# Expert layers with whole fp32 rows and results, gathered pair by pair, with a ring of twelve weight places

## The chip, the cores and the metric

One core of a Trainium2 chip runs the whole program. Its engines are TensorE (PE in the profile; PEld is its weight load), VectorE (DVE), ScalarE (ACT), GpSimd (POOL) and SyncE (SP), which issues the DMAs. The metric is the device time of one execution in microseconds.

## The reference, cut to what matters

Three transformer blocks run one after the other over 256 tokens of width 1024. Each ends in a mixture of experts: a router picks two of 32 experts for every token, and each expert is a gated two-layer product. The first block has narrow experts (hidden width 256), the two others wide ones (512).

```python
def hierarchical_moe_2(x, w_coarse, b_coarse, w_fine, b_fine, w_gate, w_up, w_down):
    ...
    order = jnp.argsort(expert_id)
    tok = order // TOP_K
    sizes = jnp.bincount(expert_id, length=N_EXPERTS_2)
    xs = xt[tok]                                             # gather
    hid = jax.nn.silu(lax.ragged_dot(xs, w_gate, sizes)) * lax.ragged_dot(xs, w_up, sizes)
    ys = lax.ragged_dot(hid, w_down, sizes) * gate.reshape(-1)[order][:, None]
    return jax.ops.segment_sum(ys, tok, num_segments=T)      # scatter
```

The narrow layer (`hierarchical_moe`) computes the same with other names. Everything is fp32. The rest of the program (projections, gated linear attention, delta rule, retention, window attention, a Fourier mixer, norms) is not changed by the diff except in where some buffers lie.

## The kernel before, in words

`stage_packed` (L1633) runs one expert layer. The 32 experts are taken as 16 pairs; each expert has 64 slots (`CAP`), so that a pair fills 128 partitions. For each pair:

- **gather** (L1693): the token rows of the pair are collected by products with a 0/1 matrix `one`. The rows `h` are kept as two tiles, `h_high` (rounded to fp32r by ACT, L1451) and `h_low` (the rest, subtracted by POOL, L1476), each the stationary operand of a product of type fp32r (L1704, L1705). One call gathers a *batch*: four pairs in the narrow layer (moving operand 512 columns), two pairs in a wide one (256 columns). That is 8 row blocks x 2 token halves x 2 parts = 32 products for each batch. ACT copies the result out of PSUM (L1795).
- **gate and up products** (`hidden`, L1708, L1717) in fp32, ACT's Silu (L1800), DVE's product of the two (L1860), a turn of the result by PE (L1769), ACT's copy of it (L1803), the **down product** (L1740).
- the result times the slot's gate is again kept as high (ACT, L1813) and low (DVE, L1870), and **scattered** (L1722): for each of four outputs of 128x512 two fp32r products (L1727, L1728), which DVE adds to `x` (L1834). The scatter of pair p stands in PE's order of pair p+1: outputs 0 and 1 behind the up product, 2 and 3 behind the turn.

PE's written order within pair p is: gate, turn of the gated one-hot (L1757), up, scatter 0 and 1 of pair p-1, turn of hidden (L1769), scatter 2 and 3, gather of the next batch if p is a batch's last pair, down.

The weights stream through a **ring** of places of 2 MB each (`Experts`, L1571). A narrow pair takes 3 such chunks (48 in the layer), a wide pair 6 (96 in the layer). SP issues chunk i when the place of chunk i - ring size has been used (L1616). The ring has 8 places in the narrow layer and 10 in a wide one. Ring places are also used by other stages: the first loads of a layer are issued wherever a place is already free, in `stage_norm`, `stage_fourier` and `stage_out_route` (L1336), the last two behind a wait for the out product (L2577), since `store` holds its weights.

`stage_out_route` computes the output projection (L1396), the residual and norm on DVE, the turned rows (L1404), the router's logits (L1412), a long chain of small DVE operations that picks the experts (L1513 to L1562), and PE's ranking product (L1431). `refine` is a Newton step for a square root.

Of the kernel before, what the change touches and what calls it, by code (L numbers as in the profile page):

```python
# [7 lines left out]
ALU = mybir.AluOpType  # L8
# [3 lines left out]
F32R = mybir.dt.float32r  # L12
I32 = mybir.dt.int32

P = 128
T = 256
# [238 lines left out]
def stage_norm_t(k, tag, src, weight, ahead=None):  # L255

    nc = k.nc
    s_w, s_ss, s_inv, s_rs, s_h, s_t = (k.sem(f"{n}_{tag}") for n in (
        "norm_weight_loaded", "sumsq_done", "inv_done", "rstd_done", "h_done", "turned"))
    scope = ExitStack()  # L260
    k.scope = scope
    ss = k.sb(f"ss_{tag}", [P, NJ])
    inv = k.sb(f"inv_{tag}", [P, NJ])
    rstd = k.sb(f"rstd_{tag}", [P, NJ])
    turned = k.ps(f"turned_ps_{tag}", [P, 4, W])
    rows, wrow = src, None
    if weight is not None:
        rows = k.sb(f"norm_rows_{tag}", [P, NJ, D])
        wrow = k.sb(f"norm_row_{tag}", [P, D])

    with scope, nc.Block() as block:
        @block.sync
        def _(sp):
            if weight is not None:
                sp.dma_start(wrow[:], weight.broadcast_to([P, D])).then_inc(s_w, 16)
            if ahead is not None:
                ahead(sp)

        @block.scalar
        def _(act):  # L280
            if weight is not None:
                for j in range(NJ):
                    nc.scalar.activation(rows[:, j, :], src[:, j, :], ACT.Square,
                                         accum_out=ss[:, j:j + 1]).then_inc(s_ss, 1)
                act.wait_ge(s_inv, 1)
                nc.scalar.activation(rstd[:], inv[:], ACT.Sqrt).then_inc(s_rs, 1)

        @block.vector
        def _(dve):
            o = Order(dve, k.order["dve"])  # L290
            if weight is not None:
                dve.wait_ge(s_ss, NJ)
                o(nc.vector.tensor_scalar(ss[:], ss[:], 1.0 / D, EPS, ALU.mult, ALU.add))
                nc.vector.reciprocal(inv[:], ss[:]).then_inc(s_inv, 1)
                dve.wait_ge(s_rs, 1)
                refine(nc, o, rstd[:], ss[:], inv[:])
                dve.wait_ge(s_w, 16)
                for j in range(NJ):
                    nc.vector.scalar_tensor_tensor(out=rows[:, j, :], in0=src[:, j, :], scalar=rstd[:, j:j + 1],
                                                   in1=wrow[:], op0=ALU.mult, op1=ALU.mult).then_inc(s_h, 1)  # L300
            for b in range(4):
                j, c0 = b // 2, 4 * (b % 2)
                dve.wait_ge(s_t, b + 1)
                dst = k.hT[:, c0:c0 + 4, j * P:(j + 1) * P]
                got = turned[:, b, :].rearrange("p (c t) -> p c t", c=4)
                nc.vector.tensor_copy(dst, got)
            o.restart()

        @block.tensor
        def _(pe):  # L310
            for b in range(4):
                j, c0 = b // 2, 4 * (b % 2)
                if weight is not None:
                    pe.wait_ge(s_h, j + 1)
                for c in range(4):
                    last = nc.tensor.transpose(turned[:, b, c * P:(c + 1) * P],
                                               rows[:, j, c0 + c:D:KC], k.table("ident"))
# [958 lines left out]
def stage_norm(k, tag, gain, bias, ahead=None, out=None):  # L1276
# [6 lines left out]
    with scope:  # L1283
        g = k.sb(f"gain_{tag}", [P, D])
        b = k.sb(f"bias_{tag}", [P, D])
        stats = k.sb(f"stats_{tag}", [P, NJ, 2, 6])
        mv, v, inv, rs = (k.sb(f"{n}_{tag}", [P, NJ, 2]) for n in ("mean_var", "var_eps", "inv", "rstd"))
        with nc.Block() as block:
            @block.sync
            def _(sp):  # L1290
                sp.dma_start(g[:], gain.broadcast_to([P, D])).then_inc(s_ld, 16)  # L1291
                sp.dma_start(b[:], bias.broadcast_to([P, D])).then_inc(s_ld, 16)
# [15 lines left out]
            def _(dve):  # L1308
# [9 lines left out]
                def rows(j):  # L1318
# [4 lines left out]
                    o(nc.vector.scalar_tensor_tensor(out=xj, in0=xj, scalar=mv[:, j, 0:1], in1=g[:],  # L1323
# [241 lines left out]


CHUNK = 2 * KC * H1
RING = 10


class Experts:  # L1571
# [1067 lines left out]
```

## Time and profile before

| | us |
|---|---|
| runs | 2005.18, 2002.22, 2004.66 (median 2004.66) |
| the profiled execution | 2002.44 |
| its span | 2000.5 |
| PE busy in the span | 1785.5 (89%) |
| DVE / ACT / POOL busy | 674.3 / 427.7 / 83.4 |
| HBM read | 577.39 MB, 290 GB/s over the span |

The narrow expert layer runs from about 554 to 808 us of the span, the first wide layer from about 986 to 1437, the second from about 1533 to 1984. PE's records of consecutive matmuls overlap, so that the spacing of their starts, and not their mean duration, tells what one costs. An fp32 product shows as two records, an fp32r product and a turn as one. An engine that waits for a DMA is shown with the tile that the DMA writes.

### The profile page before, as it was taken

The numbers are of one execution on the slowest core, as the hardware profiler recorded it, in microseconds if no ns is written. First come the engines' busy times: TensorE is split into PE (matmuls) and PEld (weight loads), VectorE is DVE, ScalarE is ACT, GpSimd is POOL, SyncE is SP. The second block draws the span as 40 slices with busy tenths as digits, with TensorE's granted clock in tenths as the row PEclk, the third lists the DMA queues.
The fourth block names the chain that finished last, engine by engine and source line by source line (L and its number), as shares of the span: only waits on it lengthen the run. The fifth ranks groups of instructions, "written<-read, shape, count | busy, mean of one in ns | idle before, by whom it ended". The sixth has DMA issues, their size and how long they took to land. (4 is left out here: it accounts for less than half of the span.)

```text
span 2000.5 us, 20692 instructions
## 1 busy us (share of the span) xinstructions
PE 1785.5 (89%) x8544; PEld 952.9 (48%) x8544; DVE 674.3 (34%) x1347; ACT 427.7 (21%) x713; POOL 83.4 (4%) x66
## 2 busy tenths in 40 slices
PE   7999897895799999799799999899597999998995
PEld 6884454695455555456434443333254344442331
DVE  3657333446223334443412222122303122221223
ACT  2321224352222221222211111111112111111110
POOL 0000001311100000120100000000001000000000
PEclk9999998797899999899799999999897999999998
DMA  5345320004669996432999999999793999999995
GB/s 194 127 162 178 123 88 4 0 1 194 243 249 398 403 419 266 144 155 73 384 423 423 423 423 423 423 424 423 299 375 143 424 423 423 423 423 424 423 423 232
DMA packets 100017, 581.49 MB, mean 291 GB/s; under 512 B 23947, under 2 KB 26251, under 8 KB 34893
## 3 DMA queue, kind: packets, MB, share of 16 engines
q1 hardware_dynamic: 87997, 577.81, 70.8%
q10 hardware_dynamic: 11920, 2.26, 0.6%
q8 instruction: 73, 1.20, 0.2%
q14 instruction: 27, 0.22, 0.0%
HBM read 577.39 MB, written 2.62 MB: 290 GB/s over the span
## 5 line engine op out<-in xcount | busy, mean ns | idle before, releaser
L1717 PE MATMUL up_ps_l<-pool,hT 128*64 128x512 f32 x640 | 143.5, 597 | 13.4 <-DMA pool<-in_expert_w_up 13.4
L1717 PE MATMUL gate_ps_l<-pool,hT 128*64 128x512 f32 x640 | 141.4, 593 | 6.6 <-DMA pool<-in_expert_w_gate 5.3
L446 PE MATMUL proj_ps<-pool,hT 128*128 128x512 f32 x320 | 140.2, 598 | 5.6 <-DVE pool L684 5.6
L1740 PE MATMUL y_ps_l<-pool,hidden_l 128*64 128x512 f32 x640 | 142.6, 596 | 2.3 <-ACT hidden_l L1803 1.4
L1870 DVE SCALAR_TENSOR_TENSOR y_low_l<-y_ps_l,slot_gate_l,y_high_l 128x512 fp32r<-128x512 f32 x64 | 47.1, 751 | 251.2 <-ACT y_high_l L1813 251.2
L438 PE MATMUL proj_ps<-hT,pool 128*128 128x256 f32 x512 | 111.9, 380 | 0.0
L1860 DVE TENSOR_TENSOR hidden_l<-hidden_l,up_ps_l 128x512 f32<-128x512 f32 x32 | 22.0, 688 | 245.2 <-PE up_ps_l L1717 245.2
L438 PEld LDWEIGHTS proj_ps<-hT,pool 128*128 128x128 f32 x512 | 96.9, 190 | 14.8 <-issue 1.8
L446 PEld LDWEIGHTS proj_ps<-pool,hT 128*128 128x128 f32 x320 | 61.4, 192 | 81.3 <-issue 74.7
L1717 PEld LDWEIGHTS gate_ps_l<-pool,hT 128*64 128x64 f32 x640 | 45.5, 137 | 98.4 <-issue 87.6
L1717 PEld LDWEIGHTS up_ps_l<-pool,hT 128*64 128x64 f32 x640 | 43.6, 137 | 99.4 <-issue 77.8
L1813 ACT ACTIVATE y_high_l<-y_ps_l,slot_gate_l 128x512 fp32r<-128x512 f32 x64 | 44.0, 687 | 203.1 <-PE y_ps_l L1740 199.6
L1740 PEld LDWEIGHTS y_ps_l<-pool,hidden_l 128*64 128x64 f32 x640 | 43.8, 137 | 88.1 <-issue 77.7
L1704 PE MATMUL gather_ps_l<-onehot_l,h_high_l 128*128 128x256 f32 x256 | 68.0, 302 | 16.9 <-DVE x L1834 12.9
L1800 ACT ACTIVATE hidden_l<-gate_ps_l 128x512 f32<-128x512 f32 x32 | 34.3, 1072 | 215.1 <-PE gate_ps_l L1717 215.1
L1803 ACT ACTIVATE hidden_l<-gate_ps_l 128x512 f32<-128x512 f32 x32 | 19.1, 598 | 277.0 <-PE gate_ps_l L1769 277.0
L1705 PE MATMUL gather_ps_l<-onehot_l,h_low_l 128*128 128x256 f32 x256 | 66.0, 295 | 0.0
L1834 DVE SCALAR_TENSOR_TENSOR x<-x,gather_ps_l 128x512 f32<-128x512 f32 x96 | 62.8, 682 | 1.7 <-PE gather_ps_l L1728 1.7
L1704 PEld LDWEIGHTS gather_ps_l<-onehot_l,h_high_l 128*128 128x128 f32 x256 | 52.1, 204 | 23.1 <-DVE x L1834 18.9
L1396 PE MATMUL out_ps_l<-store,hT 128*128 128x512 f32 x128 | 55.7, 593 | 1.7 <-PEq L2145 1.0
L1795 ACT ACTIVATE hT<-gather_ps_l 128x512 f32<-128x512 f32 x64 | 38.3, 598 | 67.1 <-PE gather_ps_l L1705 67.1
L1705 PEld LDWEIGHTS gather_ps_l<-onehot_l,h_low_l 128*128 128x128 f32 x256 | 52.2, 204 | 0.0
(503 smaller groups left out, 2682.0 us busy)
## 6 DMA issues: line engine op xcount, KB each, us to landing
pool<-in_expert_w_gate SPq DMA_DIRECT2D x40, 2048.0 KB, 32.4
pool<-in_expert_w_up SPq DMA_DIRECT2D x40, 2048.0 KB, 30.2
pool<-in_expert_w_down SPq DMA_DIRECT2D x40, 2048.0 KB, 32.1
pool<-in_w_in_blocks SPq DMA_DIRECT2D x18, 2048.0 KB, 7.7
pool<-in_moe_w_gate SPq DMA_DIRECT2D x12, 2048.0 KB, 12.6
pool<-in_moe_w_up SPq DMA_DIRECT2D x12, 2048.0 KB, 12.0
pool<-in_moe_w_down SPq DMA_DIRECT2D x12, 2048.0 KB, 11.6
gate_room<-in_expert_w_gate SPq DMA_DIRECT2D x12, 2048.0 KB, 29.9
```

The costliest lines, as they stand in the source:

```text
L438: last = mm(pp[:, n % 2, m * T:(m + 1) * T], wbuf[n % 2][:, c, m * P:(m + 1) * P], k.hT[:, c, :], start=(c == 0), stop=(c == KC - 1))
L446: last = mm(pp[:, n % 2, j * W:(j + 1) * W], k.hT[:, c, j * P:(j + 1) * P], wbuf[n % 2][:, c, :], start=(c == 0), stop=(c == KC - 1))
L1396: last = nc.tensor.matmul(y[:, j, n, :], k.hT[:, c, j * P:(j + 1) * P], w_out[:, c, n * W:(n + 1) * W], start=(c == 0), stop=(c == KC - 1))
L1704: mm(at, k.h_high[:, j, c], moving, start=(j == 0), stop=False)
L1705: last = mm(at, k.h_low[:, j, c], moving, start=False, stop=(j == NJ - 1))
L1717: last = mm(out[e * CAP:(e + 1) * CAP, 0:H], xg(part * r + c)[:, at:at + CAP], ex.weights(i, e, c), start=(part + c == 0), stop=(part == e ...
L1740: last = mm(Y[e * CAP:(e + 1) * CAP, n], hidT[:, part * r + c, e * CAP:(e + 1) * CAP], ex.weights(i, e, c)[:, n * W:(n + 1) * W], start=(p ...
L1795: nc.scalar.activation(to, got, ACT.Copy).then_inc(s_xg, 1)
L1800: nc.scalar.activation(hid[:].rearrange("p (c n) -> p n c", c=HT), G[:, 0:H].rearrange("p (n c) -> p n c", c=HT), ACT.Silu).then_inc(s_sg, 1)
L1813: nc.scalar.activation(yh[:, n], Y[:, n], ACT.Copy, scale=slot_gate[:, 0:1]).then_inc(s_yh, 1)
L1834: nc.vector.scalar_tensor_tensor(out=xs, in0=xs, scalar=1.0 if p else alpha, in1=scatter_bank[o], op0=ALU.mult, op1=ALU.add).then_inc(s_ad ...
L1870: nc.vector.scalar_tensor_tensor(out=yl[:, n], in0=Y[:, n], scalar=slot_gate[:, 0:1], in1=yh[:, n].bitcast(F32), op0=ALU.mult, op1=ALU.sub ...
```

## The change

Rows are no longer split: the fp32 tile `rows` (or `x`) serves as `k.h`, and ACT's `high` and POOL's subtraction are gone. `one`, `oneT` and the result `yh` are fp32; `yl` is gone with its DVE operation. Batches are one pair each. Outputs 0 and 1 of the scatter stand before the up product (only output 0 for the last pair), output 2 behind it, output 3 behind the gather and the turn; output 3 goes to the `Up` bank. DVE adds into a second tile `k.sum` in the wide layers. Memory that is freed becomes two more ring places for the wide layers, and three chunks of the first wide layer are issued within `stage_even`. The second wide layer has one more chunk issued in `stage_norm` and one more in `stage_fourier`.

```diff
-RING = 10
+RING = 12
...
+        self.batches = [[p] for p in range(NE // 2)]
...
                             for j in range(NJ):
-                                moving = one[:, j].rearrange("p e s -> p (e s)")
-                                mm(at, k.h_high[:, j, c], moving, start=(j == 0), stop=False)
-                                last = mm(at, k.h_low[:, j, c], moving, start=False, stop=(j == NJ - 1))
+                                moving = one[:, j].rearrange("p e s -> p (e s)")[:, 0:width]
+                                last = mm(at, k.h[:, j, c:D:KC], moving, start=(j == 0), stop=(j == NJ - 1))
...
-                    if o == 3:
-                        pe.wait_ge(s_add, 4 * p + 1)
                     to_tile = oneT[:, (o // 2) * P:(o // 2 + 1) * P]
-                    mm(scatter_bank[o], to_tile, yh[:, o % 2], start=True, stop=False)
-                    mm(scatter_bank[o], to_tile, yl[:, o % 2], start=False, stop=True).then_inc(s_sc, 1)
+                    last = mm(scatter_bank[o], to_tile, yh[:, o % 2], start=True, stop=True)
+                    last.then_inc(s_sc, 1)
...
                     last.then_inc(s_pt, 1)
+                    if p:
+                        pe.wait_ge(s_yh, 2 * p)
+                        pe.wait_ge(s_add, 4 * p - 4)
+                        for o in range(early(p)):
+                            scatter(p - 1, o)
                     hidden(p, 1, Up)
                     if p:
-                        pe.wait_ge(s_ys, 2 * p)
-                        if p > 1:
-                            pe.wait_ge(s_add, 4 * p - 4)
-                        scatter(p - 1, 0)
-                        scatter(p - 1, 1)
+                        for o in range(early(p), 3):
+                            scatter(p - 1, o)
+                    if b:
+                        if p:
+                            pe.wait_ge(s_add, 4 * p - 2)
+                        gather(b, 0, 2)
                     pe.wait_ge(s_hid, p + 1)
...
-                    if p:
-                        scatter(p - 1, 2)
                         scatter(p - 1, 3)
-                    if new_batch(p):
-                        if p:
-                            pe.wait_ge(s_add, 4 * p)
-                        gather(p // GB + 1)
...
-                def high(j):
-                    act.wait_ge(s_h, j + 1)
-                    nc.scalar.activation(k.h_high[:, j], by_chunk(j), ACT.Copy).then_inc(s_hi, 1)
...
-                    nc.gpsimd.tensor_tensor(k.h_low[:, j], by_chunk(j), k.h_high[:, j].bitcast(F32), ALU.subtract)
...
+        def early(sp, s_half):
+            ex[1].load(sp, 1)
+            for products in (8, 10):
+                sp.wait_ge(s_half, products)
+                ex[1].load(sp, 1)
...
-            ex[2].load(sp, 2)
+            ex[2].load(sp, 3)
...
-                stage_fourier(k, lambda sp: ex[2].load(sp, 4))
+                stage_fourier(k, lambda sp: ex[2].load(sp, 5))
...
-                ex[1 + n].load(sp, 2 if n else 8)
+                ex[1 + n].load(sp, 2 if n else 7)
```

## Rows read from the trace of the kernel before

**Rows 1.** Page, 40 slices of 50 us: share of the DMA engines in tenths.

```profile
DMA  5345320004669996432999999999793999999995
```

**Rows 2.** Windows: length, then busy us (count) by engine, PEclk, DMA share, GB/s.

```profile
650.00:700.00 50.00, 49.05 (x318) 28.05 (x316) 19.29 (x34) 11.95 (x20) 0.00 (x0) 1.00 0.98 404
1100.00:1150.00 50.00, 49.08 (x244) 20.61 (x242) 11.30 (x20) 7.12 (x10) 0.00 (x0) 1.00 1.01 423
1350.00:1400.00 50.00, 46.03 (x224) 18.93 (x222) 10.96 (x19) 7.08 (x10) 0.00 (x0) 1.00 1.01 423
```

**Rows 3.** Timeline, ACT's copy of the turned hidden, narrow layer: start, duration.

```profile
573.97 0.38 ACT L1803 ACTIVATE hidden_one<-gate_ps_one 128x256 f32<-128x256 f32 x1 [4.30 <-PE gate_ps_one L1769]
600.16 0.38 ACT L1803 ACTIVATE hidden_one<-gate_ps_one 128x256 f32<-128x256 f32 x1 [4.67 <-PE gate_ps_one L1769]
613.45 0.38 ACT L1803 ACTIVATE hidden_one<-gate_ps_one 128x256 f32<-128x256 f32 x1 [4.69 <-PE gate_ps_one L1769]
...
799.13 0.38 ACT L1803 ACTIVATE hidden_one<-gate_ps_one 128x256 f32<-128x256 f32 x1 [4.68 <-PE gate_ps_one L1769]
```

**Rows 4.** The same copy in the first wide layer.

```profile
1009.84 0.60 ACT L1803 ACTIVATE hidden_l<-gate_ps_l 128x512 f32<-128x512 f32 x1 [7.75 <-PE gate_ps_l L1769]
...
1062.18 0.60 ACT L1803 ACTIVATE hidden_l<-gate_ps_l 128x512 f32<-128x512 f32 x1 [7.86 <-PE gate_ps_l L1769]
1085.93 0.60 ACT L1803 ACTIVATE hidden_l<-gate_ps_l 128x512 f32<-128x512 f32 x1 [7.85 <-PE gate_ps_l L1769]
1114.68 0.60 ACT L1803 ACTIVATE hidden_l<-gate_ps_l 128x512 f32<-128x512 f32 x1 [7.86 <-PE gate_ps_l L1769]
...
1423.83 0.60 ACT L1803 ACTIVATE hidden_l<-gate_ps_l 128x512 f32<-128x512 f32 x1 [10.46 <-PE gate_ps_l L1769]
```

**Rows 5.** Window at the end of the first wide layer's loads.

```profile
1425.00:1430.00 5.00, 4.86 (x24) 1.49 (x22) 1.33 (x3) 0.00 (x0) 0.00 (x0) 1.00 0.27 115
```

**Rows 6.** Timeline, PE around a wide pair's scatter.

```profile
1060.52 0.50 PE L1727 MATMUL gather_ps_l<-y_high_l,onehot_T_l 128*128 128x512 f32 x1
...
1061.08 0.40 PE L1727 MATMUL gather_ps_l<-y_high_l,onehot_T_l 128*128 128x512 f32 x1
...
1061.55 0.60 PE L1769 MATMUL gate_ps_l<-tables,hidden_l 128*128 128x128 f32 x4
1061.90 0.47 PE L1727 MATMUL scatter_ps_l<-y_high_l,onehot_T_l 128*128 128x512 f32 x1
...
1062.99 0.65 PE L1740 MATMUL y_ps_l<-gate_room,hidden_l 128*64 128x512 f32 x2
```

**Rows 7.** Timeline, PE: fp32 products outside the expert layers.

```profile
935.41 20.84 PE L1396 MATMUL out_ps_l<-store,hT 128*128 128x512 f32 x48 [1.03 <-PEq L2145]
913.60 3.73 PE L2417 MATMUL even_mix_ps<-even_nat,pool 128*128 128x128 f32 x32
```

**Rows 8.** Lines: weight loads for turns of strided rows; count, busy us, mean ns.

```profile
L2437 PEld LDWEIGHTS even_mix_ps<-tables,even_mixed 128*128 128x128 f32 x8 | 1.0, 190 | 0.5 <-issue 0.5
```

**Rows 9.** Timeline, PE: first gather and first gate product of two layers.

```profile
555.10 0.80 PE L1704 MATMUL gather_ps_one<-onehot_one,h_high_one 128*128 128x512 f32 x1 [2.53 <-DVE onehot_one L1822]
565.33 1.95 PE L1717 MATMUL gate_ps_one<-pool,hT 128*64 128x256 f32 x16 [0.69 <-ACT gathered_T_one L1795]
986.43 0.58 PE L1704 MATMUL gather_ps_l<-onehot_l,h_high_l 128*128 128x256 f32 x1 [2.01 <-DVE onehot_l L1822]
993.88 7.09 PE L1717 MATMUL gate_ps_l<-pool,hT 128*64 128x512 f32 x32 [0.69 <-ACT hT L1795]
```

**Rows 10.** Timeline, DVE and POOL in the routing of the first wide layer.

```profile
974.51 2.84 POOL L1476 TENSOR_TENSOR h_low_l<-x,h_high_l 128x1024 fp32r<-128x1024 f32 x1 [11.83 <-ACT h_high_l L1451]
975.88 1.49 DVE L1514 TENSOR_TENSOR eq_l<-logits_l,max_l 128x8 f32<-128x8 f32 x1
977.41 0.17 DVE L1515 TENSOR_TENSOR eq_l<-eq_l,router_tables_l 128x8 f32<-128x8 f32 x1
```

**Rows 11.** Page, costliest groups: DVE's low part in the wide layers.

```profile
L1870 DVE SCALAR_TENSOR_TENSOR y_low_l<-y_ps_l,slot_gate_l,y_high_l 128x512 fp32r<-128x512 f32 x64 | 47.1, 751 | 251.2 <-ACT y_high_l L1813 251.2
```

More of the change, by code:

```diff
@@ L252, in stage_first, with stage_turn @@
     k.scope = k.ctx
-def stage_norm_t(k, tag, src, weight, ahead=None):
+def stage_turn(k, src, ahead):
     nc = k.nc
-    s_w, s_ss, s_inv, s_rs, s_h, s_t = (k.sem(f"{n}_{tag}") for n in (
-        "norm_weight_loaded", "sumsq_done", "inv_done", "rstd_done", "h_done", "turned"))
+    s_t = k.sem("mixer_turned")
     scope = ExitStack()
     k.scope = scope
[L262 to L269, printed above, removed]
+    turned = k.ps("turned_ps_mixer", [P, 4, W])
     with scope, nc.Block() as block:
@@ L273, in _ @@
         def _(sp):
[L274 to L286, printed above, removed]
+            ahead(sp)
         @block.vector
         def _(dve):
[L290 to L300, printed above, removed]
             for b in range(4):
@@ L1677, in down_used, with early @@
             return ex.used0 + (p + 1) * CP
+        def early(p):
+            return 2 if new_batch(p) else 1
         def new_batch(p):
-            return p % GB == GB - 1 and p < NI - 1
+            b, _ = ex.batch_of[p]
+            return b + 1 if p == ex.batches[b][-1] and p < NI - 1 else 0
         with nc.Block() as block:
@@ L1714, in hidden @@
                         for c in range(r):
+                            if what == 0 and q == 0 and (part * r + c) % per[b] == 0:
+                                pe.wait_ge(s_xg, groups_before[b] + (part * r + c) // per[b] + 1)
                             for e in range(2):
-                                at = (p % GB) * P + e * CAP
-                                last = mm(out[e * CAP:(e + 1) * CAP, 0:H], xg(part * r + c)[:, at:at + CAP],
+                                at = q * P + e * CAP
+                                last = mm(out[e * CAP:(e + 1) * CAP, 0:H], xg(part * r + c)[:, 0, at:at + CAP],
                                           ex.weights(i, e, c), start=(part + c == 0),
@@ L1788, in _, with gathered @@
             def _(act):
-                def gathered(b):
-                    for n in range(KC // PER):
-                        act.wait_ge(s_gx, b * (KC // PER) + n + 1)
-                        got = XG[:, n % 2].rearrange("p (m s) -> p m s", m=PER)
-                        c = n * PER
-                        to = xg_first[:, c:c + PER] if c < here else xg_rest[:, c - here:c - here + PER]
-                        nc.scalar.activation(to, got, ACT.Copy).then_inc(s_xg, 1)
-                gathered(0)
+                def gathered(b, first, end):
+                    for n in range(first, end):
+                        act.wait_ge(s_gx, groups_before[b] + n + 1)
+                        width = len(ex.batches[b]) * P
+                        got = XG[:, n % 2, 0:per[b] * width].rearrange("p (m s) -> p m s", m=per[b])
+                        nc.scalar.activation(xg(n * per[b], per[b])[:, :, 0:width], got, ACT.Copy).then_inc(s_xg, 1)
+                gathered(0, 0, groups[0])
                 for p in range(NI):
+                    b = new_batch(p)
                     act.wait_ge(ex.s_used, gate_used(p))
@@ L2065, with stage_even @@
 RD = 128
-def stage_even(k):
+def stage_even(k, early):
     nc, i = k.nc, k.i
@@ L2159, in _ @@
                         load_out(k, sp, i["w_out_even"].rearrange("(p c) n -> p c n", c=KC))
+                early(sp, s["half_product"])
             @block.gpsimd
@@ L2512, in build @@
         ex[0].ring(k.store, 2)
-        for n in range(2):
-            ex[1 + n].ring(k.pool, 6)
         rows_pc, rows_cp = "(p c) n -> p c n", "(c p) n -> p c n"
-        def split_rows(tag):
-            k.h_high, k.h_low = (k.sb(f"h_{n}_{tag}", [P, NJ, KC, P], F32R) for n in ("high", "low"))
         with ExitStack() as mixer:
```

215 lines of the change are left out of this document (107 added, 108 removed).

## The prediction

> **What bounds the kernel now.** I read the 40 slices first: through the three expert layers the DMA engines are at nine tenths or more [rows 1], which looks as if the weights paced all of it. The windows, read next, split it. In the narrow layer PE is busy 49.05 of 50 us; early in a wide layer it is 49.08; late in a wide layer it falls to 46.03 while the DMA share stays at 1.01 [rows 2]. So the narrow layer and the first half of a wide one are paced by PE, the second half of a wide one by the weights.
>
> The copy of the turned hidden, once a pair, is the clock hand. A narrow pair without a gather takes 613.45 - 600.16 = 13.29 us, and the 15 periods from the first pair's copy to the last one's take 799.13 - 573.97 = 225.2 us [rows 3]. A wide pair takes 1085.93 - 1062.18 = 23.75 us without a gather and 1114.68 - 1085.93 = 28.75 us with one for two pairs, 26.25 on average; its 15 periods take 414.0 us [rows 4]. The weights of a wide pair are six chunks of 2.097 MB; at 423 GB/s [rows 2] a chunk takes 4.96 us and a pair 29.8. PE is faster than that, so it eats up its stock of ten chunks and then waits. The second wide layer repeats this: a copy at each of the same 15 periods, 414.0 us in all.
>
> **Scatter.** Before, four outputs cost 1061.55 - 1060.52 = 1.03 us for two of them and 1062.99 - 1061.90 = 1.09 for the others, that is 2.12 us with the wait for ACT's copy in it; from 1061.08 on two fp32r records take 0.47 us, 0.23 each [rows 6]. After, each output is one fp32 product, which is two records. The out product has 48 records in 20.84 us, 0.434 each [rows 7], so an output costs 0.87 and four cost 3.47 us. The diff looks as if it halved the products; it makes 1.35 us more of each pair.
>
> **Gather.** Before, (28.75 - 23.75) / 2 = 2.5 us for each wide pair, and in the narrow layer (225.2 - 15 x 13.29) / 3 = 8.6 us for each of three batches of four pairs, 2.2 for a pair. After, each pair has 8 x 2 = 16 fp32 products of 128 moving columns. The retention product is just that, 32 records of 128x128 in 3.73 us [rows 7]; the last record's tail (an estimate, 0.16) lies beside what follows, and 3.57 us are left, 0.112 a record. The new stationary operand is strided (every eighth element). The trace has no strided fp32 product. From below it could cost as much as a contiguous one: eight turns of strided rows load their weights in 1.0 us, with 190 ns for one, so that their starts are (1.0 - 0.19) / 7 = 0.116 us apart [rows 8], as close as the records of the contiguous product. From above, the loads might not overlap in a four-pass product; then a record takes 0.19 us and the gather 6.1 us. I take 3.57, since the turn reads the very same pattern.
>
> The Trainium skill bears on this in "TensorE: Matmul & The Clock Gate", section "LDWEIGHTS (loading the stationary operand)": a load costs its columns divided by 1.2, 107 ns for 128, and layout does not enter. By that rule, an estimate, a gather would be 32 x 107 ns = 3.4 us, and the total 8 us lower than mine; it speaks against batches of one pair, since the load is paid again for each 128 columns.
>
> **The order in a pair.** The new order enters a group of products three more times than before. The first two records of a group take 1061.08 - 1060.52 = 0.56 us, where the next two take 0.47 [rows 6]: 3 x 0.1 = 0.3 us. The gather now stands before the turn of hidden, and ACT must copy its second half before it copies the turned hidden. Before, the copy started at 1062.18 and took 0.60 [rows 4], and the down product began 0.21 later [rows 6]. After, with e the end of the gather: ACT copies e + 0.2 to e + 0.8, then hidden to e + 1.45, and down may start at e + 1.65; PE has a turn (0.35) and output 3 (0.97) to do, until e + 1.35 to 1.45. That leaves a wait 0.2 us longer than before. The other waits (adds 0 and 1 before the gather, the one-hot, the product of gate and up) have the up product or the gather in front of them, 7 and 3.6 us, and cost nothing; were the cover gone, DVE's two adds would be 1.3 us.
>
> So a narrow pair takes 13.29 - 2.12 + 3.47 + 3.57 + 0.5 = 18.7 us and a wide pair 23.75 + 5.42 = 29.2.
>
> **The ring of twelve.** The last chunk of the first wide layer lands at about 1426, where the DMA share falls [rows 5]. Ten chunks fill the ring before the first place is used; the other 86 take 86 x 4.96 = 427 us, so DMA has run without a gap since the first gate product's half way, near 1000 [rows 9]. With 12 chunks in place 84 are left, and the last lands at about 1417. But PE now reaches its last chunk only 15 x 29.2 us behind its first pair, near 1446. Twelve chunks of stock are 60 us, and the stock is used at 29.8 - 29.2 = 0.6 us a pair. So DMA ends nothing any more, and the two new places and the early loads bring nothing: their cost is nothing too, since the DMA engines are at three tenths or less in the slices from 850 to 950, where the early chunks go [rows 1], and the routing loads of the second wide layer (issued 20 us before the first of their users on PE) may come 10 us later. If they did not hide, 1 us or so would be late in that norm.
>
> **The sum, against the profiled execution's 2002.44 us.**
> Fifteen periods, fourteen of them with a gather: narrow 15 x 18.7 - 3.6 = 277.0, +51.8; wide 15 x 29.2 - 3.6 = 434.1, +20.1 each. The wide layer pays less because the 16 us that PE waited for weights are filled first.
> Before the first copy: the narrow layer's first gather is 32 products of 512 columns, 555.10 to 565.33 [rows 9]. Sixteen of 128 columns take 0.445 us each at 1.2 GHz, which by the spacing of the records lasted 3.8 us there, then 0.22 each, 5.5 us in all, and DVE's one-hot is 0.8 shorter: -5.4. The second gather within the first pair adds 3.7: -1.7. Wide: 986.43 to 993.88 [rows 9], where 1.2 GHz held for 6.1 us; 6.6 us after, -1.1, and +3.7: +2.6 each.
> Routing: DVE's first comparison takes 1.49 us and ends at 977.37; its neighbour of the same shape takes 0.17. POOL's subtraction runs 974.51 to 977.35 [rows 10]. DVE is on the path there, and the subtraction goes: -1.3 for each of three layers. The Trainium skill has this in "SBUF — State Buffer", section "Who interferes with whom": a DVE instruction with two SBUF inputs is blocked for the whole of a GpSimd one that reads SBUF. By it the gain is -3.9 us, and without it zero.
> Tail of a layer: the last scatter has nothing beside it, so its 1.35 us count, and the second low part, 0.75 us behind ACT's copy [rows 11], goes: +0.6.
> Narrow: 51.8 - 1.7 - 1.3 + 0.6 = +49.4. Wide: 20.1 + 2.6 - 1.3 + 0.6 = +22.0, twice 44.0. Together +93.4, so 2095.8. The profiled execution is 2.2 below the median of the runs shown; the forecast stays at 2096, inside that.
>
> **Rivals.**
> *A. The wide layers stay with the weights.* Six chunks take 29.8 us and my wide pair 29.2, so the added PE work would hide and the ring's 2 x 9.9 us show: 2002.4 + 49.4 - 19.8 = 2032. Against it stands the stock: DMA would have to be 60 us slower over a layer. It needs a wide pair below (1417 - 1012) / 15 = 27 us. 5%.
> *B. Not slower.* If an fp32 product costs by its count of records like two fp32r ones, PE's pair stays as it is, weights pace the wide layers' second half, and twelve places take two chunks off each: -19.8, and -3.9 from POOL: 1979. It decides where gather and scatter together grow by less than 24 / 48 = 0.5 us a pair; I have 3.7 for a narrow pair and 2.9 for a wide one. Against it: 0.434 against 0.23 per record [rows 6, 7]. 3%.
> *C. Strided weights pace the gather.* If each of the 32 loads shows its whole 190 ns [rows 8], a gather takes 6.1 us in place of 3.57, and 48 of them +121: 2217. The turns' spacing speaks against it. 5%.
> *D. The forecast*, 87%. Its own width is the 0.5 us of entries and waits, which may be 0 or 1.0: 45 periods x 0.5 = 23 us on either side, 2073 to 2119.
>
> Range 2073 to 2120. A difference within 0.2%, about what a measurement of this kernel can tell from no change, has 1%; faster has 2%, slower 97%.
>
> **What would show it.** Right: 18.7 and 29.2 us between copies of the turned hidden, the same at the start and the end of a wide layer; 32 gather records in 3.6 us; no PE wait for weights; gaps in DMA within the wide layers; the first comparison of the routing near 0.17 us. Wrong: PE below 48 of 50 us in a late window with DMA at 1.01 (A), scatter outputs under 0.6 us (B), gather records more than 0.13 us apart (C), or a new wait of PE of over 1 us in each pair, most likely for ACT before the down product.

## The result, and the profile after

| | before | after |
|---|---|---|
| median, us | 2004.45 (4 runs) | 2261.61 (4 runs, 2257.91 to 2266.95) |
| profiled execution, us | 2002.44 | 2262.76 |
| its span, us | 2000.5 | 2260.9 |

The ratio after to before is 1.1287, with a 95% interval of 1.1262 to 1.1312. The direction was forecast, the size was not: 2262 lies far above the range of 2073 to 2120. Of the runs below, one of experiment 1 (8522.19 us) and one of the copy in experiment 2 (4109.61) were several times slower than their three neighbours; they are left out of the medians and ratios.

The first line of the page and the DMA line of its slices, after. In [rows 1] the DMA line has nines in the middle of the narrow layer (and sixes at its two ends) and through nearly all of the wide ones. Now it has sevens and sixes in the narrow layer (about 555 to 920 us, slices of 56.5) and a three at its end, and in the wide ones it falls off before their end:

```profile
PE 2111.5 (93%) x9440; PEld 1232.0 (54%) x9440; DVE 614.8 (27%) x1279; ACT 410.9 (18%) x707; POOL 66.4 (3%) x60
...
DMA  5344300054767673455899999996295999999960
```

The windows, to be read against [rows 2] (narrow layer, early and late in a wide one):

```profile
690.00:740.00 50.00, 50.00 (x273) 32.09 (x274) 10.96 (x21) 8.49 (x15) 0.00 (x0) 1.00 0.63 254
1150.00:1200.00 50.00, 50.00 (x221) 26.14 (x222) 6.46 (x12) 7.18 (x11) 0.00 (x0) 1.00 0.90 371
1500.00:1550.00 50.00, 50.00 (x213) 27.06 (x212) 8.60 (x15) 5.51 (x8) 0.00 (x0) 1.00 0.95 397
```

PE is busy 50.00 of 50 us in all three, and the DMA share has fallen from 1.01 to 0.90 and 0.95 in the wide layer: the weights now wait for PE, from start to end. The clock hand, ACT's copy of the turned hidden, in the narrow layer and then in the first wide one, against [rows 3, 4] (start, duration):

```profile
869.99 0.38 ACT L1773 ACTIVATE hT<-gate_ps_one 128x256 f32<-128x256 f32 x1
892.34 0.38 ACT L1773 ACTIVATE hT<-gate_ps_one 128x256 f32<-128x256 f32 x1
906.93 0.38 ACT L1773 ACTIVATE hT<-gate_ps_one 128x256 f32<-128x256 f32 x1 [6.34 <-PE gate_ps_one L1740]
...
1123.61 0.59 ACT L1773 ACTIVATE hT<-gate_ps_l 128x512 f32<-128x512 f32 x1
...
1189.28 0.59 ACT L1773 ACTIVATE hT<-gate_ps_l 128x512 f32<-128x512 f32 x1
1222.14 0.59 ACT L1773 ACTIVATE hT<-gate_ps_l 128x512 f32<-128x512 f32 x1
...
1583.60 0.59 ACT L1773 ACTIVATE hT<-gate_ps_l 128x512 f32<-128x512 f32 x1
1608.89 0.60 ACT L1773 ACTIVATE hT<-gate_ps_l 128x512 f32<-128x512 f32 x1 [9.53 <-PE gate_ps_l L1740]
```

A narrow pair with a gather takes 892.34 - 869.99 = 22.35 us, the last one, which has no gather to do, 906.93 - 892.34 = 14.59. A wide pair takes 1222.14 - 1189.28 = 32.86 with a gather and 1608.89 - 1583.60 = 25.29 without. So a gather costs 7.76 and 7.57 us, where the forecast had 3.57; without it the pairs are at 14.59 and 25.29, where the forecast had 18.7 - 3.57 = 15.1 and 29.2 - 3.57 = 25.6. PE's timeline shows the same in one step:

```profile
1147.25 1.12 PE L1693 MATMUL scatter_ps_l<-y_out_l,hT 128*128 128x512 f32 x2
1148.21 7.68 PE L1670 MATMUL gather_ps_l<-onehot_l,x 128*128 128x128 f32 x32
1155.73 0.60 PE L1740 MATMUL gate_ps_l<-tables,hT 128*128 128x128 f32 x4
1156.16 1.02 PE L1693 MATMUL up_ps_l<-y_out_l,hT 128*128 128x512 f32 x2
1157.12 1.08 PE L1706 MATMUL y_ps_l<-store,hT 128*64 128x512 f32 x4
```

The 32 records of a gather take 1155.73 - 1148.21 = 7.52 us, 0.235 each. The retention product of [rows 7], the same 32 records of the same shape with a contiguous stationary operand, took 3.73. The lines say where it shows: the weight loads of the gather, in number, busy us and mean ns, and below them its products:

```profile
L1670 PEld LDWEIGHTS gather_ps_l<-onehot_l,x 128*128 128x128 f32 x512 | 124.6, 335 | 7.7 <-issue 4.2
...
L1670 PE MATMUL gather_ps_l<-onehot_l,x 128*128 128x128 f32 x512 | 123.4, 400 | 1.7 <-DVE onehot_l L1792 1.7
```

A load takes 335 ns, where the strided load of a turn took 190 [rows 8]. And the loads' busy time, 124.6 us, is that of the products beside them: while the gather runs, the load is the pace.

### The profile page after: what moved, and what is told of

It is laid out like the page before. It is cut to its first block and busy times, and to the rows that moved or that the text cites. A ratio compares the mean times of both kernels' runs of the same rounds, so it can differ in the third digit from the quotient of the medians.

```text
span 2260.9 us, 22446 instructions
## 1 busy us (share of the span) xinstructions
PE 2111.5 (93%) x9440; PEld 1232.0 (54%) x9440; DVE 614.8 (27%) x1279; ACT 410.9 (18%) x707; POOL 66.4 (3%) x60
## 5 line engine op out<-in xcount | busy, mean ns | idle before, releaser
L1670 PEld LDWEIGHTS gather_ps_l<-onehot_l,x 128*128 128x128 f32 x512 | 124.6, 335 | 7.7 <-issue 4.2
L1670 PEld LDWEIGHTS gather_ps_l<-onehot_l,rows_other 128*128 128x128 f32 x512 | 124.2, 334 | 7.6 <-issue 4.2
L1670 PEld LDWEIGHTS gather_ps_one<-onehot_one,gate_room 128*128 128x128 f32 x512 | 124.2, 334 | 7.2 <-issue 3.7
L1670 PE MATMUL gather_ps_l<-onehot_l,x 128*128 128x128 f32 x512 | 123.4, 400 | 1.7 <-DVE onehot_l L1792 1.7
L1670 PE MATMUL gather_ps_one<-onehot_one,gate_room 128*128 128x128 f32 x512 | 122.9, 400 | 1.7 <-DVE onehot_one L1792 1.7
L1670 PE MATMUL gather_ps_l<-onehot_l,rows_other 128*128 128x128 f32 x512 | 122.9, 400 | 1.7 <-DVE onehot_l L1792 1.7
L1706 PE MATMUL y_ps_l<-pool,hT 128*64 128x512 f32 x512 | 113.4, 595 | 1.5 <-ACT hT L1773 1.5
L1706 PE MATMUL y_ps_l<-store,hT 128*64 128x512 f32 x512 | 113.4, 595 | 0.0
L1685 PE MATMUL up_ps_l<-gate_room,hT 128*64 128x512 f32 x384 | 85.9, 596 | 0.0
L1783 ACT ACTIVATE y_out_l<-y_ps_l,slot_gate_l 128x512 f32<-128x512 f32 x64 | 43.9, 687 | 209.9 <-PE y_ps_l L1706 206.4
```

Source lines behind the costliest of these rows:

```text
L1670: last = mm(at, k.h[:, j, c:D:KC], moving, start=(j == 0), stop=(j == NJ - 1))
L1685: last = mm(out[e * CAP:(e + 1) * CAP, 0:H], xg(part * r + c)[:, 0, at:at + CAP], ex.weights(i, e, c), start=(part + c == 0), stop=(part = ...
L1706: last = mm(Y[e * CAP:(e + 1) * CAP, n], hidT[:, part * r + c, e * CAP:(e + 1) * CAP], ex.weights(i, e, c)[:, n * W:(n + 1) * W], start=(p ...
L1783: nc.scalar.activation(yh[:, n], Y[:, n], ACT.Copy, scale=slot_gate[:, 0:1]).then_inc(s_yh, 1)
```

## Experiments

Each ratio is to runs of the kernel before on the same chip, with its 95% interval. Where periods or records are given, they come from the profiled execution of the kernel named, and its time is compared with the profiled 2262.76 of after and 2002.44 of before. The theories: **S**, the stride of the stationary operand; **M**, fp32 products of 128 columns in this setting, whatever the stride; **W**, some wait or neighbour of the new order.

### 1. The same gather, contiguous

```
-  last = mm(at, k.h[:, j, c:D:KC], moving, start=(j == 0), stop=(j == NJ - 1))
+  last = mm(at, k.h[:, j, c * P:(c + 1) * P], moving, start=(j == 0), stop=(j == NJ - 1))
```

The kernel thereby gathers other columns than the experts need; the number of products, their shapes and the bytes read stay.

> The changed kernel, but each gather product takes 128 neighbouring columns of the rows as its stationary operand instead of every eighth column. Everything else stays, the count of products too (the gathered values are those of other columns, so the output is not the reference's). Theory S, the stride of the stationary operand makes each weight load of an fp32 product slow: gather records 0.11 us apart as in the retention product, a narrow pair 14.6 + 3.6 = 18.2 us and a wide one 25.3 + 3.6 = 28.9 us, in all 48 x 4.1 = 195 us less than the changed kernel, about 2067. Rival M, a product of only 128 moving columns that accumulates in PSUM costs 0.24 us a record here whatever its layout: no change, 2261. Rival W, the gap is a wait on ACT or DVE that the new order brings: no change either, and the records would show a gap ahead of the group and not an even spacing.

Measured: median 2076.72, ratio 1.0365 (1.0345 to 1.0386), profiled 2077.17. PE's timeline at the same place, and the line of the loads:

```profile
1077.33 1.12 PE L1693 MATMUL scatter_ps_l<-y_out_l,hT 128*128 128x512 f32 x2
1078.30 3.73 PE L1670 MATMUL gather_ps_l<-onehot_l,x 128*128 128x128 f32 x32
1081.87 0.60 PE L1740 MATMUL gate_ps_l<-tables,hT 128*128 128x128 f32 x4
```

```profile
L1670 PEld LDWEIGHTS gather_ps_l<-onehot_l,x 128*128 128x128 f32 x512 | 61.3, 197 | 9.4 <-issue 7.5 <-DVE onehot_l L1792 1.9
```

The gather takes 1081.87 - 1078.30 = 3.57 us, to the hundredth what the forecast had, and 32 records last 3.73 as in [rows 7]. The scatter output ahead of it keeps its 0.97. Pairs are 18.43 and 28.91 us with a gather and 14.59 and 25.29 without, the last two as in after. S is shown, M and W fall. The two executions differ by 2262.76 - 2077.17 = 185.6 us. About 182 of these lie in the gathers: 165 in the 42 of the periods, and 17 in the first two of each layer. The other 3 us lie ahead of the first gather, which starts at 555.61 us after and at 552.62 here, where the stride plays no part.

### 2. A contiguous copy of the rows, and strides between

The whole computation again: ACT copies each normed half of the rows into a tile ordered by chunk, which takes the room of the twelfth place.

```
+  k.h = k.sb("rows_by_chunk_l", [P, NJ, KC, P])
+  nc.scalar.activation(k.h[:, 0], by_chunk(0), ACT.Copy)   # and 1, behind each turn
-  last = mm(at, k.h[:, j, c:D:KC], moving, ...)
+  last = mm(at, k.h[:, j, c], moving, ...)
-  RING = 12
+  RING = 11
...
```

> The changed kernel with the whole computation kept: ACT copies the fp32 rows once per half into a tile in which the 128 columns of a gather product are neighbours (two copies of about 2.1 us in each route stage, where the old kernel rounded the high part). The tile takes memory, so the wide ring has eleven places. Theory S: as with neighbouring columns, about 2067; the copies lie beside DVE's routing and cost nothing, and the twelfth place was worth nothing. If the ring mattered, it would be 5 to 10 us above the run with neighbouring columns. Rivals M and W: 2261.

Measured: median 2078.27, ratio 1.0369 (1.0348 to 1.0391), and the pairs of experiment 1, 28.91 us each (ACT's copies, start and duration):

```profile
1085.32 0.59 ACT L1777 ACTIVATE hT<-gate_ps_l 128x512 f32<-128x512 f32 x1
...
1114.23 0.59 ACT L1777 ACTIVATE hT<-gate_ps_l 128x512 f32<-128x512 f32 x1
```

So the copy (2.05 and 2.08 us of ACT for the two halves, in each of three layers) gives back 2262.76 - 2079.78 = 183.0 us, all that the gathers lost by the stride, and the twelfth place is not missed. Even then the change stays 3.7% behind the kernel before.

Two smaller strides, with everything else as in experiment 1: every second column (8 bytes), and every fourth (16 bytes).

```
-  last = mm(at, k.h[:, j, c:D:KC], moving, ...)
+  last = mm(at, k.h[:, j, c:c + 2 * P:2], moving, ...)      # stride_2
+  last = mm(at, k.h[:, j, c:c + 4 * P:4], moving, ...)      # e11_stride_4
```

> The changed kernel with every second column (stride of 8 bytes) as stationary operand of the gather, instead of every eighth (32 bytes); the gathered columns are others, so the output is not the reference's. If the cost is that of any stride other than one: 2261. If it grows with the stride or comes from the 32 bytes: near 2067, or between.

> The changed kernel with every fourth column (16 bytes) as the gather's stationary operand; the gathered columns are others, so the output is not the reference's. Stride 1 gave records 0.12 us apart, stride 2 about 0.13, stride 8 0.24. If the cost grows with the stride: between 0.13 and 0.24, 2100 to 2200 in all. If it begins at 32 bytes: 0.13, about 2087.

Measured in one profiled execution each: 2086.99 and 2258.72. The loads at 8 bytes:

```profile
L1670 PEld LDWEIGHTS gather_ps_l<-onehot_l,x 128*128 128x128 f32 x512 | 64.8, 202 | 9.3 <-issue 7.4 <-DVE onehot_l L1792 1.9
```

and at 16 bytes:

```profile
L1670 PEld LDWEIGHTS gather_ps_l<-onehot_l,x 128*128 128x128 f32 x512 | 121.8, 328 | 7.7 <-issue 4.2 <-DVE onehot_l L1792 1.9
```

A gather at 8 bytes, in PE's timeline:

```profile
1080.48 3.95 PE L1670 MATMUL gather_ps_l<-onehot_l,x 128*128 128x128 f32 x32
1084.28 0.60 PE L1740 MATMUL gate_ps_l<-tables,hT 128*128 128x128 f32 x4
```

At 8 bytes a load takes 202 ns and a gather 1084.28 - 1080.48 = 3.80 us, 0.119 a record; at 16 bytes they are at 328 ns and 1155.20 - 1147.86 = 7.34 us, 0.229 a record, nearly the 335 ns and 7.52 us of the change's 32 bytes. The cost sets in between 8 and 16 bytes and hardly grows from 16 to 32. All operands here have 4-byte elements, so that bytes and elements are not told apart.

### 3. Is it fp32, is it the clock, and why not the turn?

First the kernel before with its high and low rows in the order in which they come, so that its fp32r gather reads every eighth element:

```
-  mm(at, k.h_high[:, j, c], moving, ...)
-  last = mm(at, k.h_low[:, j, c], moving, ...)
+  mm(at, k.h_high[:, j, c:D:KC], moving, ...)
+  last = mm(at, k.h_low[:, j, c:D:KC], moving, ...)
...
```

> The kernel before, with the high and low tiles laid out in the natural order of the rows, so that its fp32r gather products read their stationary operand with the same stride of eight. If any strided load of 128 columns takes 0.24 us: the 32 records of a wide batch go from 0.12 to 0.24 us apart, +3.9 us for each of 16 batches, of which the 16 us of waiting for weights in each layer hide half: 2004 + 30 = 2034; the narrow layer's records (512 columns, 0.23) hide it nearly. If only four-pass fp32 products suffer: no change, 2004.

Measured: median 2011.47, ratio 1.0046 (1.0029 to 1.0062). The loads of the gather in that kernel:

```profile
L1705 PEld LDWEIGHTS gather_ps_l<-onehot_l,h_low_l 128*128 128x128 f32 x256 | 86.6, 338 | 0.0
L1704 PEld LDWEIGHTS gather_ps_l<-onehot_l,h_high_l 128*128 128x128 f32 x256 | 86.1, 336 | 23.1 <-DVE x L1834 18.9 <-DVE onehot_l L1822 4.3
```

and in the kernel before:

```profile
L1705 PEld LDWEIGHTS gather_ps_l<-onehot_l,h_low_l 128*128 128x128 f32 x256 | 52.2, 204 | 0.0
L1704 PEld LDWEIGHTS gather_ps_l<-onehot_l,h_high_l 128*128 128x128 f32 x256 | 52.1, 204 | 23.1 <-DVE x L1834 18.9 <-DVE onehot_l L1822 4.3
```

From 204 ns to 336 and 338: the fp32r product suffers the same. The copies around a gather of two pairs, strided:

```profile
1089.29 0.60 ACT L1803 ACTIVATE hidden_l<-gate_ps_l 128x512 f32<-128x512 f32 x1 [7.86 <-PE gate_ps_l L1769]
...
1121.93 0.60 ACT L1803 ACTIVATE hidden_l<-gate_ps_l 128x512 f32<-128x512 f32 x1 [7.87 <-PE gate_ps_l L1769]
```

1121.93 - 1089.29 = 32.6 us, where [rows 4] have 28.75: 3.9 more for each of the seven gathers within the 15 periods, 27.3 in all. But the 15 periods take 418.5 us in place of 414.0. Before, PE had 414.0 - 8 x 23.75 - 7 x 28.75 = 22.75 us of waits for weights in a wide layer; 27.3 - 22.75 = 4.6, and 4.5 is what shows. The periods of this run alternate between 23.75 and 32.65 to the layer's end, so that PE has no such wait left. Where moving columns are 512 (a batch of four narrow pairs) most of the load hides: 22.77 us for that step in place of 22.02, 0.02 more a record. I had expected 2034 here. That let only 16 us of waits hide the loads where there are 22.75, and it charged a layer's first gather 3.9 too, which in the first wide layer grew by only 1.2 (8.66 us for 7.45): most of it runs at a granted clock of 0.50 in both kernels, and at that clock the stride costs little (below). This is the point that the change gives up: fp32 products of 128 moving columns have nothing to hide such a load behind, in a layer that PE paces.

Then the turn, the place from which the price was taken. In the kernel before, the turns of the normed rows are written as fp32 products with the identity; the tile, the stride and the counts stay:

```
-  last = nc.tensor.transpose(turned[...], rows[:, j, 4 * n + c:D:KC], k.table("ident"))
+  last = nc.tensor.matmul(turned[...], rows[:, j, 4 * n + c:D:KC], k.table("ident"), start=True, stop=True)
```

> The kernel before, with the eight turns of each half's rows in the three route stages done as fp32 products with the identity, from the same tile, with the same stride and the same identity, in place of the transpose mode. A product shows two records. If strided loads are slow in any product and fast in a turn: 16 records 0.24 us apart, at either granted clock. If the slow loads came from where the gather's rows or its moving operand lie: 0.11 us apart at 2.4 GHz and 0.22 at 1.2.

Measured in one profiled execution: 2013.52. As products:

```profile
960.89 3.84 PE L1404 MATMUL turned_ps_l<-tables,x 128*128 128x128 f32 x16
...
977.47 4.19 PE L1404 MATMUL out_ps_l<-tables,x 128*128 128x128 f32 x16 [4.15 <-DVE x L1509]
```

As turns, before:

```profile
956.08 1.05 PE L1404 MATMUL turned_ps_l<-tables,x 128*128 128x128 f32 x8
...
969.86 1.97 PE L1404 MATMUL out_ps_l<-tables,x 128*128 128x128 f32 x8 [4.15 <-DVE x L1509]
```

Eight turns take 1.05 us; the same eight operands as products are sixteen records and take 3.84. Twice the records explain twice the time, not 3.7 times: a record is 0.24 us from the next, and its load takes 332 to 335 ns in place of the turn's 190. The same data with the same stride is cheap in transpose mode and dear in a product. That the turn too loads the rows as its stationary operand is read from the order of the names (`tables,x` in both, moving operand first, as in the gather's `onehot_l,x`); the records hold no addresses that would show it. Why the turn escapes stays open. The second group of products ran at 1.2 GHz (a granted clock of 0.50 from 977.50 to 981.50), the first at 2.4: 4.19 against 3.84 us, 0.25 and 0.24 a record. The turns themselves took 1.97 against 1.05. So the strided load hardly follows PE's clock. The first gather of the first wide layer after shows that too, here in the timeline:

```profile
1092.93 7.91 PE L1670 MATMUL gather_ps_l<-onehot_l,x 128*128 128x128 f32 x32 [1.74 <-DVE onehot_l L1792]
```

and in windows over its two halves (columns as in [rows 2]):

```profile
1093.00:1097.00 4.00, 4.00 (x17) 4.00 (x18) 0.95 (x5) 0.00 (x0) 0.00 (x0) 0.50 0.99 410
1097.00:1100.80 3.80, 3.80 (x19) 3.68 (x18) 0.00 (x0) 0.60 (x1) 0.00 (x0) 0.98 0.04 17
```

With the clock at 0.50 for its first 4.07 us, this gather lasts 7.91 us, and the one at full clock that starts at 1148.21 lasts 7.68. At a pace set by the clock, those 4.07 us would have done the work of 2.04, and the whole would have taken 7.68 + 2.04 = 9.7 us. The contiguous load does follow the clock. In experiment 1's kernel, the loads at the start of the narrow layer's first gather and the window over the same stretch:

```profile
L1670 PEld LDWEIGHTS gather_ps_one<-onehot_one,gate_room 128*128 128x128 f32 x17 | 3.7, 330 | 1.9 <-DVE onehot_one L1792 1.9
```

```profile
552.62:556.00 3.38, 3.38 (x16) 3.38 (x17) 1.03 (x5) 0.00 (x0) 0.00 (x0) 0.50 0.00 0
```

Here 16 records take 3.38 us, 0.21 each, and a contiguous load takes 330 ns, where at full clock it is 0.112 and 192 to 204. So at 1.2 GHz a strided record costs little more than a contiguous one (0.24 to 0.25 us for 0.21), and at 2.4 GHz twice as much (0.235 for 0.112).

### 4. What the rest of the change is worth

Both from experiment 1's kernel. The ring back to ten, without the loads behind the out product:

```
-  RING = 12
+  RING = 10
...
-  sp.wait_ge(s_out, 4)
-  ex[1 + n].load(sp, 2)
```

> The run with neighbouring columns (output not the reference's), with ten ring places for the wide layers; the chunks behind the out product are not loaded early. If PE paces the wide layers throughout (28.9 us a pair against 29.8 of weights, with ten chunks in stock, 50 us, of which 15 x 0.9 = 14 are used): the same time as with twelve, about 2067. If the twelfth place mattered: 10 to 20 us more.

Measured: median 2075.24, ratio 1.0369 (1.0354 to 1.0384). The two places are worth nothing here. Windows late in the first wide layer, of this kernel:

```profile
1360.00:1410.00 50.00, 50.00 (x254) 21.88 (x252) 7.84 (x14) 7.19 (x11) 0.00 (x0) 1.00 1.01 425
```

PE is busy 50.00 of 50 us beside a DMA share of 1.01: six chunks take 29.6 us at 425 GB/s and a pair 28.91, so that each pair takes 0.7 us from the stock and neither a ring of ten nor one of twelve runs out in 16 pairs.

The scatter's two early outputs put back behind the up product:

```
 def early(p):
-    return 2 if new_batch(p) else 1
+    return 0
```

> The run with neighbouring columns (output not the reference's), with scatter outputs 0, 1 and 2 all behind the up product as before the change, and output 3 behind the turn. DVE's two adds are then due between the up product and the gather: scatter 1 ends 0.87 us before the gather would start, DVE does the product of gate and up first (0.7) and then the adds (0.7 each), so PE may wait up to 0.7 us in each pair: +0 to +30 us over the run with neighbouring columns. If the order brought nothing: the same.

Measured: median 2087.56, ratio 1.0432 (1.0417 to 1.0447); pairs 18.62 and 29.10. The line of the loads has a new wait for DVE's add, 10.5 us in a layer:

```profile
L1670 PEld LDWEIGHTS gather_ps_l<-onehot_l,x 128*128 128x128 f32 x512 | 59.9, 196 | 13.2 <-DVE rows_other L1804 10.5 <-DVE onehot_l L1792 1.9 <-issue 0.8
```

So the scatter around the up product is worth 0.19 us a pair: the 15 periods of each layer are 2.6 us longer, 7.8 in all. The profiled executions differ by 10.5. The rest lies mostly before the first narrow copy (574.2 for 571.2 us), where the first gather alone starts 4.5 us later (557.10 for 552.62), and the order of the scatter plays no part in that.

### 5. The ring where it counts: the kernel before

If the weights end a wide layer before, a place more should show there. The kernel before, with an eleventh place; its room comes from a smaller reserve for dynamic DMAs and from a leaner first turn.

```
-  RING = 10
+  RING = 11
+  k.spare_room = k.sb("spare_room", [P, 1 * CHUNK])
+      ex[1 + n].ring(k.spare_room, 1)
-  nc = bacc.Bacc("TRN2", target_bir_lowering=False, num_devices=1)
+  nc = bacc.Bacc("TRN2", target_bir_lowering=False, num_devices=1, dynamic_dma_scratch_size=128)
...
```

> The kernel before (split rows, batches, its order of products) with a ring of eleven places for the wide layers, the eleventh from memory reserved for GpSimd's DMA descriptors, which the kernel does not use; one more chunk is issued ahead of each wide layer. If prefetched weights are worth time only where weights pace the layer's end: DMA is idle before the first place of each wide layer is used and then runs without a gap to its end, so each layer ends one chunk of 4.96 us sooner: 2004 - 10 = 1994. If PE's own pace had become the end already: no change, 2004.

Measured: median 1983.15, ratio 0.9905 (0.9891 to 0.9919). That is 17.9 us under the kernel before on the same chip (2001.05), where 10 had been expected; the wide layers' 15 periods are 405.5 and 404.9 us, for 414.0. The part that I had not expected is in the windows, here of this kernel:

```profile
1200.00:1400.00 200.00, 187.82 (x900) 74.18 (x896) 44.63 (x75) 29.89 (x42) 0.00 (x0) 1.00 1.01 427
```

and of the kernel before:

```profile
1200.00:1400.00 200.00, 183.02 (x874) 72.04 (x872) 43.18 (x73) 28.48 (x40) 0.00 (x0) 1.00 1.01 423
```

The same DMA share moves 427 GB/s in place of 423. So the reserve was tried alone:

```
-  nc = bacc.Bacc("TRN2", target_bir_lowering=False, num_devices=1)
+  nc = bacc.Bacc("TRN2", target_bir_lowering=False, num_devices=1, dynamic_dma_scratch_size=128)
```

> The kernel before with nothing changed but the memory reserved for GpSimd's DMA descriptors (smaller, so that other buffers lie at other addresses). The eleven-place version moved 427 GB/s in the wide layers where the kernel before moved 423, which is worth about 4 us a layer beside the 5 us of the chunk. If the reserve or the addresses bring the rate: 427 GB/s and about 1995. If the eleventh place brings it: 423 GB/s and 2002.

```profile
1200.00:1400.00 200.00, 185.31 (x888) 72.82 (x884) 44.53 (x75) 29.85 (x42) 0.00 (x0) 1.00 1.01 427
```

Measured: median 1994.05, ratio 0.9954 (0.9939 to 0.9970); 409.9 us for the first wide layer's periods. The rate comes with the reserve and gives 4.1 us a layer; the eleventh place, by difference, the other 4.4 (409.9 - 405.5) in the first wide layer and 4.9 in the second, near one chunk's 4.96. The reserve also shifts where the tiles lie, and whether it is that or the reserve itself was not told apart.

Last, the one part of the change that costs nothing, taken to this kernel: the second low part is subtracted by DVE, so that POOL doesn't stand beside the first comparison.

```
-  for j in range(NJ): ... nc.gpsimd.tensor_tensor(k.h_low[:, j], by_chunk(j), k.h_high[:, j].bitcast(F32), ALU.subtract)
+  nc.gpsimd.tensor_tensor(k.h_low[:, 0], ...)          # POOL: the first half only
+  dve.wait_ge(s_hi, 2)
+  tt(k.h_low[:, 1], by_chunk(1), k.h_high[:, 1].bitcast(F32), ALU.subtract)
```

> As the eleven-place version, and the second low part of the rows is subtracted by DVE, which is idle for 5.5 us before the logits come, instead of by POOL. Theory of the shared port: DVE's first comparison falls from 1.49 to 0.17 us; the subtraction ends about 0.3 us after the logits are there; 1.0 us less in each of three layers, 1991. In the wide layers this stage lies before the first place of the ring is used, so it shows there too. Rival, the 1.49 us belong to that instruction: 0.9 us more in each layer, 1997.

```profile
972.05 2.01 DVE L1492 TENSOR_TENSOR h_low_l<-x,h_high_l 128x1024 fp32r<-128x1024 f32 x1 [4.63 <-ACT h_high_l L1416]
974.43 0.17 DVE L1478 TENSOR_TENSOR eq_l<-logits_l,max_l 128x8 f32<-128x8 f32 x1
```

Measured: median 1980.99, ratio 0.9906 (0.9891 to 0.9922). The comparison is back at 0.17 us, but the time isn't told apart from the 1983.15 without it. Both versions with the eleventh place are about 0.9% faster than the kernel before.

## Why the prediction was wrong

The forecast can be followed by sections, in us of the profiled executions (copies of the turned hidden as marks; after and experiment 1 from their 48 copies each):

| section | before | forecast | contiguous gather | after |
|---|---|---|---|---|
| start to first narrow copy | 574.0 | 571.0 | 571.2 | 579.5 |
| 15 narrow periods | 225.2 | 277.0 | 272.6 | 327.5 |
| to the first wide copy | 210.7 | 212.6 | 209.8 | 216.7 |
| 15 periods, first wide layer | 414.0 | 434.1 | 430.0 | 485.3 |
| to the next one's first copy | 132.8 | 134.7 | 132.3 | 137.9 |
| 15 periods, second wide layer | 414.0 | 434.1 | 430.0 | 484.9 |
| to the end of the span | 29.9 | 30.5 | 29.3 | 29.3 |

The last two columns differ by 185.6 us, and columns two and three by 18.6 the other way. The miss of 167 is the difference of the two.

**The step that failed: Gather.** It priced the strided stationary operand by the turn, "since the turn reads the very same pattern", at 0.112 us a record. Pattern and data were the same, the mode wasn't. A product with that stride takes 0.235 us a record and 7.52 us a gather, where contiguous it is 3.57, and 48 gathers at 3.95 more would be 190 us. The 42 within the periods are 3.92 to 3.95 more each and come to 165 us. The six at the layers' starts add 17, less than six times 3.95, since three of them run partly at a granted clock of 0.50; 3 us of the 185.6 are not the gathers'. The upper bound, a load's whole 190 ns, was taken from the same rows of turns [rows 8] and was too low for the same reason: the load itself takes 335 ns in a product. So even the dearest gather that the forecast considered, 6.1 us and a total of 2217, fell short of the measured one, and both bounds of that price hung on one row of another kind of operation. The stated range covered only the half microsecond of entries and waits, and not this price. The trace of before has no strided product at all, which the forecast said, and then did not let weigh: rival C had 5%.

Three smaller readings were off as well. [rows 1] have sixes and not nines at both ends of the narrow layer. PE's waits for weights in a wide layer were 22.75 us by [rows 4], not 16. And 7.45 us less 6.6 for the first wide gather is 0.85, where the sum has 1.1. None of them matters beside the gather.

The rule that was cited from the Trainium skill, "TensorE: Matmul & The Clock Gate", section "LDWEIGHTS (loading the stationary operand)", puts a load at its columns divided by 1.2, 107 ns here, and has no term for the layout; an estimate by it was 3.4 us a gather. The contiguous gather's 3.57 agrees with it, the strided one's 7.5 doesn't, and the measurement decides. I had used the rule as support for the lower price, where it had no strided product behind it either.

**Rival C** was right in its mechanism (strided weights pace the gather; its sign was records more than 0.13 us apart) and wrong in its price: 0.19 a record gives 2217, the measured 0.24 gives 48 x 32 x (0.235 - 0.112) = 189 us more than a contiguous gather, beside the 185.6 measured.

**Scatter: right.** An fp32 output, two records, takes 1148.21 - 1147.25 = 0.96 us up to the next group, and 1157.12 - 1156.16 = 0.96 behind the turn of hidden: the 0.87 and the 0.1 of an entry.

**The order in a pair: 0.3 us too dear.** Without a gather the pair is 14.59 and 25.29, forecast 15.1 and 25.6. Experiment 8 shows what the order is for: with the two outputs behind the up product a pair is 0.19 us longer, on DVE's adds. With a gather, contiguous, 18.43 and 28.91 for 18.7 and 29.2; 45 periods x 0.28 = 12.6 of the 18.6 us. The 0.2 us of waiting for ACT before the down product did not come: in after PE waits for that copy only in the first pair of each layer, 0.74 us each time. The range allowed for this, since it let the 0.5 us of entries and waits be anything from 0 to 1.

**The ring of twelve: right.** Ten places do as well (2075.24 against 2076.72), and PE waits for no weight in after. One sign that was given for it was not: "gaps in DMA within the wide layers" do not follow from pairs of 29.2 us and six chunks of 29.8. Experiment 4 shows the share at 1.01. The gaps of after (0.90 and 0.95) come from the longer pair.

**Routing and tail.** The subtraction on POOL is gone, and the first comparison took 0.17 us in after as forecast, where [rows 10] had 1.49:

```profile
1083.77 0.16 DVE L1460 TENSOR_REDUCE max_l<-logits_l 128x2 f32<-128x8 f32 x1
1083.97 0.17 DVE L1461 TENSOR_TENSOR eq_l<-logits_l,max_l 128x8 f32<-128x8 f32 x1
```

The rule of the Trainium skill in "SBUF — State Buffer", "Who interferes with whom", agrees with it, in experiment 6 too. That this is worth 1.3 us a layer was not shown by itself: in experiment 6, DVE does a subtraction in its place. The stretches between the layers came out 2.8, 2.4 and 1.2 us shorter than forecast in the contiguous version, the other third of the 18.6. These stretches hold the tail, the routing and the first gathers. The first gather is 5.55 and 6.38 us in the two wide layers for the forecast's 6.6, which accounts for 1.05 and 0.2 of them; the rest I did not split.

**Rivals A and B** fell: no wait of PE in after is for a DMA within the expert layers, and no output of the scatter takes less than 0.86 us.

## What to carry to other kernels

Keep the stationary operand of a product contiguous, or its elements at most 8 bytes apart, above all where the moving side is short (128 columns in fp32, 256 in fp32r); one copy per layer by an idle engine (here 4.1 us of ACT) gave back 183 us. Price an operation by a row of the same operation in the same mode: the same data, shape and stride cost twice as much a record in a product as in a turn, and a product has two records. When no such row exists, the upper bound must not come from the row that gave the lower one. Two fp32r products of a split operand (0.23 us each at 512 columns) were cheaper on PE than one fp32 product (0.87), and a ring place was worth about its chunk (4.4 and 4.9 us) in a layer that the weights end, and nothing in one that PE paces.

## What the hardware showed that I had not expected

- A load of 128 stationary columns whose elements lie 16 or 32 bytes apart takes 326 to 338 ns; a record is 0.23 (16 bytes, fp32) to 0.24 us (32 bytes, fp32 and fp32r) from the next. In fp32 it is 202 ns and 0.119 us at 8 bytes, and contiguous 197 to 200 ns and 0.112; a contiguous fp32r load takes 198 to 204 ns. In transpose mode at 32 bytes it is 190 ns and 0.116 us.
- That pace hardly follows PE's clock: 0.25 us a record at 1.2 GHz, 0.24 at 2.4. A contiguous one costs 0.21 at 1.2 GHz and 0.112 at 2.4, so that the stride costs much only at full clock.
- The kernel before moved its weights at 427 GB/s in place of 423 with a smaller reserve for dynamic DMAs, and was 0.46% faster by that alone. The cause is open.
